# Two experts' weights each in their own place in a mixture-of-experts encoder block, and another order for the first rows of the output projection

## The reference

```
h = RMSNorm(x);  p = h @ w_in                     # lru_x | lru_gate | hyena v, x1, x2, 512 columns each
y_lru = RG-LRU(conv(lru_x)) * gelu(lru_gate)       # two directions, 512 channels
y_hy  = x2 * longconv(x1 * longconv(v))            # FFT convolutions, 512 channels
x = x + concat(RMSNorm(y_lru), RMSNorm(y_hy)) @ w_out
x = x + MoE(RMSNorm(x))                            # top 1 of 4 groups, then top 2 of its 8 experts
out = RMSNorm(x)

# MoE: 4096 (token, expert) pairs, sorted by expert, each expert's list padded to blocks of 128 rows
a = silu(xb @ w1[e]) * (xb @ w3[e])                # xb [128, 1024], w1 and w3 [1024, 512]
yb = a @ w2[e]                                     # w2 [512, 1024]
y[token] += yb * gate
```

## Time and profile before

| | |
|---|---|
| median of 3 runs | 2204.33 us (2204.15 to 2205.18) |
| the profiled execution, its own time | 2205.14 us |
| its span in the profile | 2203.4 us |
| mean granted clock of TensorE | 0.952 |
| busy share PE, PEld, DVE, ACT, POOL | 90%, 64%, 55%, 48%, 37% |
| output projection | 972 to 1234 us |
| routing, first product of the experts | 1234 to 1286 us |
| experts | 1286 to 2157 us |

### The profile page before, as it was taken

How to read it: one execution, slowest core, us unless ns; L and a number is a source line. 1 busy time by engine, 2 the same in 40 slices (tenths; PEclk the granted TensorE clock), 3 DMA queues, 4 the chain that set the end, 5 groups by cost and what they waited for, 6 DMA issues and landing times. The chain is left out here.

```text
span 2203.4 us, 29377 instructions
## 1 busy us (share of the span) xinstructions
PE 1992.9 (90%) x8823; PEld 1400.6 (64%) x8824; DVE 1215.2 (55%) x1134; ACT 1063.0 (48%) x1283; POOL 812.6 (37%) x525
## 2 busy tenths in 40 slices
PE   3998999999999987979999389999998999999990
PEld 2436778777666321327777268888786888888870
DVE  6653223224666844744444656566867666665644
ACT  6871222225566431433333145565757565555634
POOL 0690000000000220321221155577877866775650
PEclk9998999999999998979999679999999999999995
DMA  6691222321233988966542358788989987887858
GB/s 219 240 326 42 77 67 77 85 81 38 60 79 99 354 297 330 357 210 224 184 153 99 150 172 269 212 303 293 380 303 373 375 292 243 306 293 223 299 150 324
DMA packets 206334, 476.88 MB, mean 216 GB/s; under 512 B 23569, under 2 KB 86165, under 8 KB 201111
## 3 DMA queue, kind: packets, MB, share of 16 engines
q1 hardware_dynamic: 165080, 383.61, 47.5%
q0 software_dynamic: 17824, 58.79, 11.5%
q10 hardware_dynamic: 23360, 33.56, 4.8%
HBM read 355.25 MB, written 114.29 MB: 213 GB/s over the span
## 5 line engine op out<-in xcount | busy, mean ns | idle before, releaser
L1923 PE MATMUL p<-wh_hi,x_hi 128*128 128x512 f32 x768 | 312.1, 406 | 18.4 <-DVE wh_lo L2055 10.7
L1869 POOL DMA_INDIRECT xg<-scratch_H,curidx x196 | 285.6, 1457 | 89.4 <-issue 45.7
L1923 PE MATMUL p<-wh_hi,x_lo 128*128 128x512 f32 x768 | 306.8, 399 | 0.0
L1923 PE MATMUL p<-wh_lo,x_hi 128*128 128x512 f32 x768 | 306.7, 399 | 0.0
L2055 DVE TENSOR_TENSOR wh_lo<-w_raw,wh_hi 128x2048 fp32r<-128x2048 f32 x128 | 284.7, 2285 | 25.3 <-ACT wh_hi L1999 25.3
L540 PE MATMUL ps<-h_hi,wp_hi 128*128 128x512 f32 x640 | 257.4, 402 | 4.3 <-DVE wp_lo L735 4.3
L540 PE MATMUL ps<-h_lo,wp_hi 128*128 128x512 f32 x640 | 254.2, 397 | 0.0
L540 PE MATMUL ps<-h_hi,wp_lo 128*128 128x512 f32 x640 | 254.0, 397 | 0.0
L1999 ACT ACTIVATE wh_hi<-w_raw 128x2048 fp32r<-128x2048 f32 x128 | 234.0, 1903 | 0.0
L1888 POOL TENSOR_TENSOR wy_lo<-w_raw,wy_hi 128x2048 fp32r<-128x2048 f32 x31 | 181.3, 5850 | 83.0 <-ACT wy_hi L2002 82.7
L1923 PEld LDWEIGHTS p<-wh_hi,x_hi 128*128 128x128 f32 x768 | 146.5, 191 | 55.6 <-DVE wh_lo L2055 11.5
(11 more groups left out here) (337 smaller groups left out, 3600.0 us busy)
## 6 DMA issues: line engine op xcount, KB each, us to landing
w_raw<-in_exp_w_dram SPq DMA_DIRECT2D x384, 512.0 KB, 7.2
dec<-in_decay_dram SPq DMA_DIRECT2D x32, 512.0 KB, 5.6
scratch_KA<-work SPq DMA_DIRECT2D x32, 512.0 KB, 4.4
scratch_SI<-arena SPq DMA_DIRECT2D x32, 512.0 KB, 4.0
kin<-scratch_KA SPq DMA_DIRECT2D x21, 512.0 KB, 6.9
arena<-scratch_SA SPq DMA_DIRECT2D x21, 512.0 KB, 5.9
wp_raw<-in_w_in_dram SPq DMA_DIRECT2D x18, 512.0 KB, 3.7
h_raw<-in_x_dram ACTq DMA_DIRECT2D x4, 2048.0 KB, 20.0
```

The source lines that it names most:

```text
L1869: pool.indirect_dma_start(out=xg[:, j, :], out_offset=None, in_=quarter_rows, in_offset=bass.IndirectOffsetOnAxis(ap=cur[:, j:j + 1], axis ...
L1923: mm = pe.matmul(acc[:, :], x[:, k, :], w, start=(k == 0 and i == 0), stop=(k == n - 1 and i == 2))
```

## The change

In the output projection the loads of `yt` and `ia` go ahead of those of `stage` and `gate`. For the first tile, PE makes the first 12 matmuls of `half(0, 0)` before `collect(0)` and the other 12 after it; ACT rounds `yt` before it squares it, and DVE subtracts it before it applies the gate. In the experts the staging place is gone. Two experts' weights have places of their own (r = 0, 1), where a load lands in the place of the low parts and is subtracted there. SP loads w2 of expert e+2 when w2 of expert e has been used (`y_done`), and behind it w1 and w3 of expert e+3 when those of e+1 have been used (`used`); the loads of the second expert wait for the first gather. The raw a takes the place of s1, and the space for descriptors of POOL's DMAs is 2048 bytes in each partition, where it was left at its default.

```diff
+            load_y(0)
+            sp.dma_start(ia[:, :], dram["inv_a"]).then_inc(ia_in, 16)
             load_stage(0)
             load_gate(0)
-            sp.dma_start(ia[:, :], dram["inv_a"]).then_inc(ia_in, 16)
-            load_y(0)
             load_x(0)
...
             pe.wait_ge(ones_ready, 1)
+            pe.wait_ge(ya_split, 1)
+            half(0, 0, pA, projA, range(1))
             pe.wait_ge(ia_in, 16)
             collect(0)
+            half(0, 0, pA, projA, range(1, 2))
             turn_z(0)
             for t in range(NT):
...
-                pe.wait_ge(ya_split, t + 1)
-                at_least(pe, xa_ready, 2 * t)
-                half(t, 0, pA, projA)
+                if t:
+                    pe.wait_ge(ya_split, t + 1)
+                    pe.wait_ge(xa_ready, 2 * t)
+                    half(t, 0, pA, projA)
...
             def first_half(t):
                 s = t % 2
                 act.wait_ge(y_in[t % 4], 16 * (t // 4) + 16)
+                at_least(act, projB, 2 * t - 2)
+                act.activation(y_hi[:, s, 0, :], yt[:, t % 4, :], ACT.Copy).then_inc(ya_round, 1)
                 at_least(act, ssq_mm, t - 1)
                 act.activation(sq[:, s, :], yt[:, t % 4, :], ACT.Square).then_inc(sq_ready, 1)
-                at_least(act, projB, 2 * t - 2)
-                act.activation(y_hi[:, s, 0, :], yt[:, t % 4, :], ACT.Copy).then_inc(ya_round, 1)
...
+            split_a(0)
             apply_gate(0)
-            split_a(0)
             split_b(0)
...
-        raw_in = [sem(f"raw_in{r}") for r in range(PAIRS)]
+        raw_in = [[sem(f"raw_in{r}_{pair}") for pair in range(PAIRS)] for r in range(2)]
...
-        raw = sb("w_raw", [P, SLABS, D])
-        wh = [sb("wh_hi", [P, KC, D], F32R), sb("wh_lo", [P, KC, D], F32R)]
-        wy = [sb("wy_hi", [P, 2 * FT, D], F32R), sb("wy_lo", [P, 2 * FT, D], F32R)]
+        wh_lo, wh_raw = in_place(nc, ctx, "wh", [P, 2, H_PAIRS, 4, D_EXP])
+        wy_lo, wy_raw = in_place(nc, ctx, "wy", [P, 2 * FT, D])
+        wh_hi = sb("wh_hi", [P, 2, H_PAIRS, 4, D_EXP], F32R)
+        wy_hi = sb("wy_hi", [P, 2 * FT, D], F32R)
...
-            with sp.Fori(0, N_EXP) as e:
-                for pair in range(PAIRS):
-                    if pair < D_PAIRS:
-                        sp.wait_ge(lowered, BASE + (e - 1) * D_PAIRS + pair + 1)
-                    else:
-                        sp.wait_ge(lowered_last, BASE + e)
...
+            def load_h(e, r, ends=None):
+                for pair in range(H_PAIRS):
+                    if ends is not None:
+                        sp.wait_ge(used, BASE + ends * KC + 2 * pair + 2 - KC)
+                    for c, name in enumerate(("exp_w1", "exp_w3")):
...
+            def load_y(e, r, ends=None):
+                if ends is not None:
+                    sp.wait_ge(y_done, BASE + ends + 2)
+                for k in range(FT):
...
+            load_h(0, 0)
+            load_y(0, 0)
+            sp.wait_ge(marks["idx_set"], BASE + 2)
+            sp.wait_ge(xg_in, 64)
+            load_h(1, 1)
+            load_y(1, 1)
+            load_h(2, 0, ends_of(0))
+            with sp.Fori(0, N_EXP // 2 - 2) as e2:
+                for r in range(2):
+                    load_y(e2 * 2 + r + 2, r, ends_of(e2 * 2 + r))
+                    load_h(e2 * 2 + r + 3, 1 - r, ends_of(e2 * 2 + r + 1))
+            load_y(N_EXP - 2, 0, ends_of(N_EXP - 4))
+            load_h(N_EXP - 1, 1, ends_of(N_EXP - 3))
+            load_y(N_EXP - 1, 1, ends_of(N_EXP - 3))
...
             def split_w(e, B, r, some=range(PAIRS)):
                 for pair in some:
-                    act.wait_ge(raw_in[pair], BASE + (e + 1) * 32)
+                    act.wait_ge(raw_in[r][pair], BASE + (e - r) * 16 + 32)
                     if pair < H_PAIRS:
-                        act.wait_ge(used, BASE + B * KC + j + 2 - KC)
-                        act.activation(by_part(wh[0], j), slabs[:, pair], ACT.Copy).then_inc(rounded, 1)
+                        hi, raw = (w[:, r, pair] for w in (wh_hi, wh_raw))
                     else:
-                        act.wait_ge(y_done, BASE + B + 1)
...
+                    act.activation(hi, raw, ACT.Copy).then_inc(rounded, 1)
...
-                act.activation(s1[:, :], p1[:, :], ACT.Silu).then_inc(s_ready, 1)
+                act.activation(a[:, :], p1[:, :], ACT.Silu).then_inc(s_ready, 1)
...
-    nc = _bacc.Bacc("TRN2", target_bir_lowering=False, num_devices=1)
+    nc = _bacc.Bacc("TRN2", target_bir_lowering=False, num_devices=1, dynamic_dma_scratch_size=2048)
```

More of the change, by code:

```diff
@@ L1361, in turn_z, with half @@
                 last.then_inc(z_turned, 1)
-            def half(t, part, banks, done):
-                for c in range(2):
+            def half(t, part, banks, done, columns=range(2)):
+                for c in columns:
                     for k in range(4):
@@ L1781, in experts @@
         nblk, idx, spot, weight, xT = yield sem
-        marks["raw_at"] = -(-nc.sbuf_base // 32) * 32
-        raw = sb("w_raw", [P, SLABS, D])
-        slabs = raw.rearrange("p s d -> p (s d)").rearrange("p (r c t f) -> p r c t f", c=2, t=2, f=D_EXP)
-        marks["wh_at"] = -(-nc.sbuf_base // 32) * 32
-        wh = [sb("wh_hi", [P, KC, D], F32R), sb("wh_lo", [P, KC, D], F32R)]
-        marks["wy_at"] = nc.sbuf_base
-        wy = [sb("wy_hi", [P, 2 * FT, D], F32R), sb("wy_lo", [P, 2 * FT, D], F32R)]
+        marks["low_at"] = -(-nc.sbuf_base // 32) * 32
+        wh_lo, wh_raw = in_place(nc, ctx, "wh", [P, 2, H_PAIRS, 4, D_EXP])
+        wy_lo, wy_raw = in_place(nc, ctx, "wy", [P, 2 * FT, D])
+        marks["high_at"] = nc.sbuf_base
+        wh_hi = sb("wh_hi", [P, 2, H_PAIRS, 4, D_EXP], F32R)
+        marks["wy_at"] = nc.sbuf_base - 4 * KC * D
+        wy_hi = sb("wy_hi", [P, 2 * FT, D], F32R)
         marks["wy_end"] = nc.sbuf_base
@@ L1794, in experts @@
         x_hi, x_lo = sb("x_hi", [P, KC, P], F32R), sb("x_lo", [P, KC, P], F32R)
-        s1, a = sb("s1", [P, D_EXP]), sb("a", [P, D_EXP])
+        a = sb("a", [P, D_EXP])
         a_hi, a_lo = sb("a_hi", [P, FT, P], F32R), sb("a_lo", [P, FT, P], F32R)
@@ L1804, in experts, with per_block @@
         x_turned = xT.rearrange("p (j k b) -> p k j b", j=4, k=KC)
-        by_part = lambda w, j: w[:, j:j + 2, :].rearrange("p t (c f) -> p c t f", c=2)
         by_j = lambda x: x.rearrange("p k (j b) -> p k j b", j=4)
-        def per_block(eng, name, body, following=None, following_last=None, on=lambda e, r: None):
+        def per_block(eng, name, body, following=None, following_last=None, on=None):
             B = eng.alloc_register(f"block_{name}")
@@ L1815, in blocks_of @@
                 with eng.Fori(0, n):
-                    body(e, eng.snap(B))
-                    on(e, r)
+                    if on:
+                        body(e, eng.snap(B), r)
+                        on(e, r)
+                    else:
+                        body(e, eng.snap(B))
                     eng.reg_add(B, B, 1)
@@ L1840, in _ @@
         def _(sp):
-            with sp.Fori(0, N_EXP) as e:
-                for pair in range(PAIRS):
-                    if pair < D_PAIRS:
-                        sp.wait_ge(lowered, BASE + (e - 1) * D_PAIRS + pair + 1)
-                    else:
-                        sp.wait_ge(lowered_last, BASE + e)
[L1847 to L1855, removed]
+            def load_h(e, r, ends=None):
[3 more added lines that the diff above has]
+                    for c, name in enumerate(("exp_w1", "exp_w3")):
+                        src = dram[name].rearrange("o e (p k) f -> p (o e) k f", p=P)[:, ds(e, 1), 2 * pair:2 * pair + 2]
+                        sp.dma_start(wh_raw[:, r, pair, 2 * c:2 * c + 2, :].rearrange("p a f -> p (a f)"), src.rearrange("p a k f -> p (a k) f")).then_inc(raw_in[r][pair], 16)
@@ new lines, in load_y, with ends_of @@
+            def load_y(e, r, ends=None):
+                if ends is not None:
+                    sp.wait_ge(y_done, BASE + ends + 2)
+                for k in range(FT):
+                    src = dram["exp_w2"].rearrange("o e (k p) f -> p (o e) k f", p=P)[:, ds(e, 1), k]
+                    sp.dma_start(wy_raw[:, r * FT + k, :], src.rearrange("p a f -> p (a f)")).then_inc(raw_in[r][H_PAIRS + k // 2], 16)
+            def ends_of(e):
+                return sp.value_load(nblk[0:1, 1, ds(e, 1)], min_val=1, max_val=N_BLOCKS)
@@ L1886, in split_last @@
                 pool.wait_ge(rounded, BASE + e * PAIRS + PAIRS)
-                hi, lo = (v[:, r * FT + 2:r * FT + 4, :] for v in wy)
-                pool.tensor_tensor(lo, raw[:, SLABS - 2:SLABS, :], hi.bitcast(F32), ALU.subtract).then_inc(lowered_last, 1)
+                hi, lo, raw = (v[:, r * FT + 2:r * FT + 4, :] for v in (wy_hi, wy_lo, wy_raw))
+                pool.tensor_tensor(lo, raw, hi.bitcast(F32), ALU.subtract).then_inc(lowered_last, 1)
             def added(B):
@@ L1942, in y @@
                     for c in range(2):
```

(35 more changed lines are left out.)

## The result

2247.39 us, median of 4 runs (2244.73 to 2251.51), against 2204.24 before: 1.0193 times as long, 95% interval 1.0181 to 1.0204. The profiled execution has a span of 2244.1 us, 40.7 more than before. It was forecast 10 slower; the direction was right and the size was a quarter of the truth.

A forecast was written before the change was run, and what follows sets the result against it. PE, busy 90% of the span, was taken as the bound, so only its idle or low-clock time could be won. Terms -5.3 - 2.7 + 14.5 + 5.4 - 2.0 = +9.9 on 2205.1 gave 2215.0, stated as 2214 by the median; range 2196 to 2225.

The forecast's parts named there:

- Start of the output projection: Output projection: `yt` loaded first lets the first matmul into pB start at 989.4 instead of 994.70; -5.3 us.
- First gather: Before the experts: holding the second expert's loads lets the first gather land sooner; -2.7 us, bounds 0 and -2.9.
- The new wait: Behind one-block experts: w2 lands at T+15.6 (T: end of p), delaying `y`; +14.5 us, bounds +6 and +25.
- Seven pay: Of fifteen experts behind a one-block expert, seven lose 1.9 us each, 13.3 in all; late x hides six.
- The clock: PE's clock falls after three of seven w2 gaps, 1.8 us each; +5.4 us, bounds 0 and +13.
- all seven gaps: Rival: PE's clock falls at every one of the seven w2 gaps, +7.2 us more, 2222 us; chance 0.11.
- The gathers: Experts: POOL's last gather issue shortens, so late gathers land about 1 us sooner in three blocks; -2.0 us.
- Costed at nothing: In-place subtraction, Silu into a, lost `used` and `y_done` waits on ACT, and w1 and w3 order: zero cost.
- w2 comes in time: Rival: w2's second pair lands by T+13.5 and a_lo is ready with p's end; 2196 us, chance 0.29.
- POOL runs out of room: Rival: with 2048 descriptor bytes each gather waits for the one before to land; 2260 us or more, chance 0.04.
- issues above 2.3 us: Sign that the forecast is wrong: POOL's issues taking longer than 2.3 us.

The follow-up runs named there:

- gate: Kernel before, with only the w2 loads of an expert held until PE has used w2 of the expert two before; 2244.1 us, ratio 1.0183.
- late3: Changed kernel with w2 split inside the expert's own first block, behind a_hi and yb on ACT, DVE subtracting all (first expert excepted); 2191.5 us, ratio 0.9933.
- hold: Changed kernel with w1 and w3 loads held until the gather under way has landed and x is transposed; 2231.9 us, ratio 1.0126.
- gate_all: Kernel before with later w2 loads, new output projection start, held second-expert loads and 2048-byte descriptor space, but old staging and places; 2233.1 us, ratio 1.0133.
- scratch: Kernel before with only the DMA descriptor space cut to 2048 bytes; 2212.7 us, ratio 1.0037.
- late: Changed kernel with ACT, DVE and POOL splitting w2 inside the expert's own first block, POOL behind scatter and gather; 2236.4 us, ratio 1.0145.
- late2: Changed kernel with w2 split in the expert's own first block, POOL subtracting between scatter and gather, first expert's w2 split at the start; 2222.9 us, ratio 1.0080.
- front_gather: Kernel before with only the new output projection start and second-expert loads held for the first gather; 2199.4 us, ratio 0.9972.

## Why the prediction was right in sign and wrong in size

- **Start of the output projection,** -5.3: right, -5.35 at the matmul that the forecast named (989.35, forecast 989.4). `yt` landed 2.7 us after issue, forecast 2.9. That the two agree to 0.1 us is luck: in the eight traces with this front the matmul starts between 986.87 and 992.24, in the three without it between 994.70 and 996.14. At the first gather's issue 4.70 of it are left.
- **First gather,** -2.7: right, -3.07. Together -7.77 at the first p.
- **The new wait,** +14.5: this is the step that failed. Place and landing were right: the second pair lands at T+15.8, forecast T+15.6. Its size was wrong twice. One gap: `y` waits not only for a_lo but for the two yb copies, which ACT does behind a_hi; in the chain 0.58, 1.16 and 0.63 us follow upon the rounding, so that pyy starts at T+19.97, not T+19.2, and a listed gap is 2.9 us in the mean (37.2 / 13), not 1.9. The count: "Seven pay" should have been thirteen. The forecast had a late x take up w2's delay in six cases. It is the other way round: `y` comes before the next p in PE's order, so PE meets w2's wait first, and the gather lands during it. None of the three waits of the earlier trace rows is left in its old size; the largest in after is 1.9 us. Of the fifteen only two come off with less than 0.6 us. 37.2 us in the place of 14.5, shown again by gate (35.7) and taken away by late3. A part of it hangs on the loads of w1 and w3: with these held back (hold) 30.0 are left.
- **The clock,** +5.4: the mechanism was right, the number of times wasn't. Nine of the products behind a gap took 7.27 to 7.96 us from first to last matmul, where the others took 5.77: some 15 us. The length of the gap alone doesn't tell which: 2.18 us was followed by the low level, 2.77 and 2.92 were not. The rival "all seven gaps" was nearer in kind.
- **The gathers,** -2.0: it was more. The three old waits and the low clock behind them were 10.7 and 6.5 us (p of 13.90, 13.01 and 14.00 against 11.46); in after waits before p, with what PE's sequencer adds, are 9.9, none followed by a long p. So -7.3. What the forecast named is there: the last issue of a block takes 1.31 us in the mean instead of 1.63, 0.96 at 1448.49 where the earlier trace rows have 1.90. That the gaps above give the gathers the rest of the time is argued; late3, without such gaps, has none above 1.4 us either, but there POOL no longer subtracts.
- **Sum as measured:** -7.8 + 38.0 (37.2 and 0.8 at the two others) + 15.2 - 7.3 + 0.7 (a slower first p) = 38.8 of the 40.7 of the span; 1.9 stay without a place.
- **Costed at nothing:** the in-place subtraction and Silu into a stand in late3 and cost nothing that its lists show. The order of w1 and w3 was not nothing: gate_all and hold put some 14 us on their earlier loads, which run beside the gathers and w2; these are inside the waits of the sum above and not beside them. The forecast had looked only at when they are wanted.
- **Rivals.** "w2 comes in time" is out. "POOL runs out of room" was given 0.04 as a matter of a whole landing for each gather; scratch shows it as 1.0 us more ahead of each block's third issue, in the mean, 7 us in the kernel before. The forecast's sign for it, issues above 2.3 us, could not tell: twelve of 196 are in after, fourteen were in the kernel before. The Trainium skill, SBUF — State Buffer, section SBUF size: 192, 224, or 256?, says what the space is for; that an eighth of it isn't free of cost, the run shows.

The Trainium skill, SBUF — State Buffer, section SBUF: two separate sides, has the port pair that VectorE and GpSimd share as an exclusive lock, held for a whole instruction. That agrees with late and late2: 11.09 us for three wh_lo, 7.38 for one wy_lo, with POOL's 5.80 and 5.19 us beside them. In after none of DVE's subtractions is longer than 2.3 us: where the two met, DVE had started 0.2 to 0.3 us sooner, and it was POOL's that took 6.5 us instead of 4.6.

## What to carry to other kernels

Before a buffer is merged with another to save staging, find out when its last reader ends and what stands in program order behind the wait for its reload, on the engine that splits it and on every engine that waits for that one: here eight us of landing sat in front of a_hi and yb, which had nothing to do with it. Moving the split of w2 behind what others wait for (late3) made a loss of 1.9% a gain of 0.7% with the same loads, where the front alone gives 0.3% (front_gather). When two waits meet in one loop, ask which of them the bounding engine reaches first: that one is paid in full, and it is the other that shrinks.

## What the runs showed of the hardware that was not expected

- A subtraction of VectorE beside one of GpSimd didn't slow by a share. The 23 long ones of late and late2 (2.7 to 7.4 us, alone 2.3) all ended 2.15 to 2.16 us after GpSimd's, which is about their own length. The other way round, with VectorE some 0.25 us sooner, GpSimd's took 6.5 us instead of 4.6, in the kernel before already (20 of 31).
- With 2048 bytes for descriptors POOL's wait ahead of gather issues grew from 45.7 to 94.3 us in all, and the growth stands at one issue of four, the third behind the scatter-add.
- In after, POOL's queue had 31.0% and SP's 68.3% of 16 engines in T+8 to T+10, where the earlier trace rows show 96.9% for POOL's, on which the forecast had leaned; w2 landed at the forecast time all the same.
